# One-hots of the gate spreading shared with GpSimd, key blocks in halves between token groups

## The chip, the cores and the metric

One core of one Trainium2 chip runs the program. The metric is device time in microseconds, the median of several executions. The kernel is written in a low-level language in which each engine has its own instruction stream and waits on semaphores explicitly; nothing reorders what is written. The engines are TensorE (PE), VectorE (DVE), ScalarE (ACT), GpSimd (POOL) and SyncE (SP), which here only issues transfers.

## The reference

It is two sublayers of a decoder for 512 prompt tokens and 32 sample tokens, 544 in all. The first (attention and a state-space mixer) is not touched. The second, PEER, retrieves 16 of 16384 experts for each of 8 heads and token:

```python
def peer_ffn(h, w_q, sub_keys, u_tab, v_tab):
    ...
    s1 = jnp.einsum('nhk,ek->nhe', q[:, :, 0], sk[0])
    s2 = jnp.einsum('nhk,ek->nhe', q[:, :, 1], sk[1])
    v1, i1 = lax.top_k(s1, PEER_TOPK)
    v2, i2 = lax.top_k(s2, PEER_TOPK)
    ...
    expert = jnp.take_along_axis(cidx, top_i, axis=-1)
    gate = jax.nn.softmax(top_s, axis=-1).astype(h.dtype)
    ...
        act = jax.nn.gelu(jnp.einsum('nd,nhkd->nhk', t, u_tab[e]), approximate=False)
        return jnp.einsum('nhk,nhkd->nd', g * act, v_tab[e])
```

An expert's number is 128 a + b, with a the first and b the second key. All is float32.

## The kernel before

384 of the tokens (three tiles of 128) are done densely. For each of the 128 values of a (a "key block") the kernel computes gelu(h U_a) for all 128 experts of the block and all 384 tokens ("up"), writes it to a table `act` in HBM, and later multiplies it with the gates and with V_a ("value"). The other 128 prompt tokens and the 32 sample tokens are done sparsely: their chosen rows of U and V are gathered from HBM (160 gathers of 128 rows of 4 KB for U, 160 for V) and combined on VectorE, a `dot` (L1750) per row of U and a `weighted_row` (L1754) per row of V.

**Up.** A block is 24 matmuls (L188 to L190: high and low halves of both operands, three products, eight chunks). SyncE fetches its 512 KB into `uraw[s]`, one of four slots (`fetch`, L1613); ScalarE casts the high half (`hi_of`, L1390); GpSimd, for the first 83 blocks, or VectorE (L1779) subtracts the low half; TensorE multiplies into bank s; ScalarE applies Gelu (`gelu`, L1662) and SyncE stores the result (`keep`, L1617). 80 blocks run beside the top-k search, and then the slab stage begins.

**Slab stage.** The gates lie as lists (a, b, gate) per token; the value stage wants a dense table gate[b, a, token]. For each token TensorE multiplies two one-hot matrices, `hot_b` (slot against b, times the gate; L1774) by `hot_a` (slot against a; L1773). Four tokens share a bank and form a token group w; there are 96. VectorE makes all one-hots in two buffers (`w % 2`), TensorE writes bank 4 or 5, ScalarE copies the bank into a slab in SBUF (L1695), and when the eight groups of 32 tokens are there SyncE stores the slab, 2 MB, to the table `gate` in HBM (`keep_slab`, L1629). There are 12 slabs. Between the groups TensorE still runs key blocks: four per slab, each followed by two groups (`slab_rows`), 48 in all. VectorE has, per block, two groups of one-hots, the low half of the block three ahead, and one dot (`quarter`). Each engine runs its list in order, so ScalarE's copies stand behind its cast of the block that SyncE fetched after the slab's store.

**Gathers.** GpSimd issues the gathers (L1605) into a ring of eight buffers; each waits until the dot or weighted row of the buffer's last use is done. In the slab stage the ring is filled at once and then four rows per slab are dotted; 16 more follow behind the last slab.

**Value stage.** For each block SyncE loads V_a, and per four blocks the stored activations and gates (`sp_rows`, `sp_gelus`, `sp_gates`). VectorE multiplies activations with gates, splits both operands, and does two sparse rows per block (`pair`); ScalarE casts; TensorE does 18 matmuls of 512 columns. It starts when the last slab is stored and its gates are read back.

The order is written out by hand everywhere; there is no planner. Semaphores count groups: `hot_ready` and `g_done`, `g_kept` tie VectorE, TensorE and ScalarE.

Of the kernel before, what the change touches and what calls it, by code (L numbers as in the profile page):

```python
# [15 lines left out]
P = 128  # L16
# [132 lines left out]
def layer(nc, t):  # L149

    ctx = ExitStack()
    with ctx:
# [1424 lines left out]
        assert EARLY + SLABS * GRP == PK  # L1577
# [8 lines left out]
        hot_ready, g_done, g_kept = (sem(n) for n in ("hot_ready", "g_done", "g_kept"))  # L1586
# [6 lines left out]
        UROWS = SLOTS + SLOTS_S  # L1593

        def pool_gather(pool):
# [4 lines left out]
            for g in range(2 * UROWS):  # L1600
                table, j = tables[g // UROWS], g % UROWS
                at = rows3[:, j:j + 1] if j < SLOTS else rowsS[:, j - SLOTS:j - SLOTS + 1]
                if g >= RING:
                    pool.wait_ge(row_done, g - RING + 1)
                pool.indirect_dma_start(gring[g % RING], None, table, bass.IndirectOffsetOnAxis(ap=at, axis=0)).then_inc(row_in[g % RING], 16)  # L1605

        def sp_up(sp):
# [21 lines left out]
            def keep_slab(n, s):  # L1629
                sp.wait_ge(g_kept, n * GS + (GS + 2))  # L1630
                sp.dma_start(t["gate"][bass.ds(n, 1)].rearrange("s p a n -> p (s a) n"), slab[s]).then_inc(slab_stored[s], 16)

            def last_rows(n, first=False, more=True):
                for s in range(4):
                    if more:
                        a = n * 4 + (EARLY + s + 4)
                        fetch(a, s, (u_lo, QF + EARLY + s + 1) if first and s < LEAD else (u_lo2, n * 4 + (s + 1 - LEAD)))
                    keep(n * 4 + (EARLY + s), s, n + EARLY // 4)

            last_rows(0, True)  # L1640
            with sp.Fori(0, (SLABS - 2) // 2) as x:
                for s in range(2):
                    keep_slab(x * 2 + s, s)
                    last_rows(x * 2 + (s + 1))
            keep_slab(SLABS - 2, 0)
            last_rows(SLABS - 1, more=False)
# [7 lines left out]
            keep_slab(SLABS - 1, 1)  # L1654

        def act_up(act):
# [3 lines left out]
            act.sem_inc(g_kept, 2)  # L1660
# [26 lines left out]
            def last_rows(n, sl, more=True):  # L1687
                for s in range(4):
                    a, q = n * 4 + (EARLY + s), n + EARLY // 4
                    gelu(a, s, q)  # L1690
                    if more:
                        hi_of(act, s, q + (QF // 4 + 1))
                    for par in range(2):
                        act.wait_ge(g_done, n * GS + (2 * s + par + 3))
                        act.copy(slab[sl][:, :, 8 * s + 4 * par:8 * s + 4 * par + 4].rearrange("p a n -> p n a"),  # L1695
                                 bank[:, 4 + par, :].rearrange("p (n a) -> p n a", a=P)).then_inc(g_kept, 1)

            with act.Fori(0, SLABS // 2 - 1) as x:
                for sl in range(2):
                    act.wait_ge(slab_stored[sl], x * 16 + 16)  # L1700
                    last_rows(x * 2 + sl, sl)
            for sl in range(2):
                act.wait_ge(slab_stored[sl], 16 * (SLABS // 2))
                last_rows(SLABS - 2 + sl, sl, sl == 0)


        def pe_up(pe):
# [26 lines left out]
            def slab_rows(n, first=False):  # L1734
                for s in range(4):
                    low = (u_lo, QF + EARLY + s + 1) if first and s < LEAD else (u_lo2, n * 4 + (s + 1 - LEAD))
                    up(n * 4 + (EARLY + s), s, low)
                    for par in range(2):
                        w = n * GS + (2 * s + par)
                        pe.wait_ge(hot_ready, w + 1)  # L1740
                        pe.wait_ge(g_kept, w + 1)
                        for j in range(4):
                            mm = pe.matmul(bank[:, 4 + par, j * P:(j + 1) * P], hot_b[:, par, j], hot_a[:, par, j], start=True, stop=True)  # L1743
                        mm.then_inc(g_done, 1)

            slab_rows(0, True)
            with pe.Fori(1, SLABS) as n:
                slab_rows(n)
# [10 lines left out]
        SLAB_ROWS = SLABS * 4  # L1759

        def dve_onehots(dve):
# [4 lines left out]
            def quarter(x, n2, s, last):  # L1766
                m = x * 8 + (4 * n2 + s)
                for par in range(2):
                    w = x * (2 * GS) + (n2 * GS + 2 * s + par)
                    dve.wait_ge(g_done, w + 1)  # L1770
                    for j in range(4):
                        at = lambda row: slotT[:, row, bass.ds(w * 4 + j, 1)]
                        dve.tensor_scalar(hot_a[:, par, j], const("iota"), at(0), None, ALU.is_equal)  # L1773
                        mm = dve.tensor_scalar(hot_b[:, par, j], const("iota"), at(1), at(2), ALU.is_equal, ALU.mult)  # L1774
                    mm.then_inc(hot_ready, 1)
# [339 lines left out]
```

## Time and profile before

| | |
|---|---|
| median of 3 runs | 2459.61 us (2459.4 to 2464.25) |
| profiled execution | 2450.02 us, span 2448.2 us |
| TensorE matmul busy | 2136.1 us (87%) |
| VectorE busy | 1589.4 us (65%) |
| ScalarE busy | 745.8 us (30%) |
| GpSimd busy | 802.8 us (33%) |
| mean granted TensorE clock | 0.931 |
| moved by DMA | 682.70 MB, mean 279 GB/s |

Shares are of the span of one profiled execution, on the only core. The engines run side by side, so busy times do not add up to the span; where one waits for another is seen in the waits and the timeline of a stretch.

### The profile page before, as it was taken

The page shows a single profiled execution, that of the slowest core. Times are in us where ns is not written, and L with a number is a line of the kernel's source. Part 1 is how long each engine was busy: PE and PEld are TensorE (multiplying, and loading weights), DVE is VectorE, ACT ScalarE, POOL GpSimd, SP SyncE. Part 2 cuts the span into 40 slices and gives each one's busy share as a digit, 9 for nine tenths or more (in the row PEclk, how much of TensorE's full clock was granted, in tenths as well). Part 3 has the DMA queues.
Part 4 walks back from the last instruction along what each step waited for, and adds up shares of the span by engine and source line. Part 5 has one row for each costly group of instructions (what it writes and reads, how often), then busy time and mean ns, then how long its engine had stood idle before and what let it go on. Part 6 is the DMA issues. An engine that isn't in the chain of part 4 may idle for free.

```text
span 2448.2 us, 36552 instructions
## 1 busy us (share of the span) xinstructions
PE 2136.1 (87%) x12253; PEld 1777.8 (73%) x12253; DVE 1589.4 (65%) x3547; ACT 745.8 (30%) x1111; POOL 802.8 (33%) x499
## 2 busy tenths in 40 slices
PE   7978999998769979999999888888399898988984
PEld 7978985554433449999999888888377676776763
DVE  1256125555352331299988677877699898988988
ACT  2123113433330012244344444444132232322231
POOL 2323310001100013366666511111444345665650
PEclk9999998999879989999999998998699899999997
DMA  9999987876995462155555666766899999999992
GB/s 350 352 355 355 356 307 307 325 298 214 325 332 180 165 213 79 43 176 170 173 169 173 218 236 230 251 236 232 322 373 394 391 395 393 395 394 394 395 389 100
DMA packets 200412, 682.70 MB, mean 279 GB/s; under 512 B 18432, under 2 KB 84352, under 8 KB 194304
## 3 DMA queue, kind: packets, MB, share of 16 engines
q1 hardware_dynamic: 151696, 508.36, 58.1%
q0 software_dynamic: 46080, 167.79, 18.1%
q10 hardware_dynamic: 2544, 5.48, 0.6%
q8 instruction: 38, 0.62, 0.1%
q14 instruction: 54, 0.44, 0.1%
HBM read 618.78 MB, written 196.32 MB: 333 GB/s over the span
## 4 chain that ended last, share of the span: by engine, by line
PE 35%; issue 22%; DMA 22%; DVE 12%; ACT 3%; POOL 3%; SPq 1%; DVEq 0%; ACTq 0%; POOLq 0%
DMA overlay<-peer_v 13%; PE bank L188 8%; PE bank L189 8%; PE bank L190 8%; DMA overlay<-peer_u 5%; DVE arena L1757 4%; PE bank L1743 2%; DVE overlay L1912 2%; POOL overlay L341 2%; PE bank L602 2%; POOL overlay L1401 2%; PE bank L586 2%; DVE arena L1752 1%; DMA overlay<-w_in 1%; PE bank L652 1%
## 5 line engine op out<-in xcount | busy, mean ns | idle before, releaser
L188 PE MATMUL bank<-overlay 128*128 128x384 f32 (+4 forms) x2856 | 987.7, 346 | 156.4 <-DVE overlay L1915 109.2
L189 PE MATMUL bank<-overlay 128*128 128x384 f32 (+4 forms) x2856 | 971.5, 340 | 0.0
L190 PE MATMUL bank<-overlay 128*128 128x384 f32 (+4 forms) x2856 | 968.6, 339 | 0.0
L188 PEld LDWEIGHTS bank<-overlay 128*128 128x128 f32 x2856 | 559.2, 196 | 211.7 <-issue 128.4
L190 PEld LDWEIGHTS bank<-overlay 128*128 128x128 f32 x2856 | 557.5, 195 | 33.6
L189 PEld LDWEIGHTS bank<-overlay 128*128 128x128 f32 x2856 | 559.1, 196 | 31.0
L1401 POOL TENSOR_TENSOR overlay<-overlay 128x1024 fp32r<-128x1024 f32 x99 | 268.1, 2711 | 205.7 <-ACT overlay L1393 205.5
L1605 POOL DMA_INDIRECT arena<-peer_rows,arena x160 | 167.3, 1046 | 447.5 <-DVE arena L1752 429.4
L1605 POOL DMA_INDIRECT arena<-peer_v,arena x160 | 236.3, 1477 | 168.8 <-DVE arena L1757 151.5
L1752 DVE SCALAR_TENSOR_TENSOR arena<-arena 128x1024 f32<-128x1024 f32 x160 | 193.9, 1216 | 17.3 <-DMA arena<-peer_rows,arena 17.2
L1757 DVE SCALAR_TENSOR_TENSOR arena<-arena 128x1024 f32<-128x1024 f32 x160 | 204.0, 1275 | 0.0
L1854 ACT CAST overlay<-overlay 128x1024 fp32r<-128x1024 f32 x128 | 134.1, 1048 | 159.3 <-DMA overlay<-peer_v 152.0
L1393 ACT CAST overlay<-overlay 128x1024 fp32r<-128x1024 f32 x144 | 150.6, 1048 | 102.2 <-DMA overlay<-peer_u 99.8
L1912 DVE TENSOR_TENSOR overlay<-overlay 128x1024 fp32r<-128x1024 f32 x128 | 155.6, 1216 | 37.5 <-ACT overlay L1854 37.5
L341 POOL TENSOR_TENSOR overlay<-overlay 128x1024 fp32r<-128x1024 f32 x44 | 104.8, 2393 | 225.8 <-ACT overlay L315 225.8
L1856 ACT CAST overlay<-overlay 128x384 fp32r<-128x384 f32 x128 | 65.7, 513 | 319.3 <-DVE overlay L1908 319.3
L1743 PE MATMUL bank<-arena 128*128 128x128 f32 x768 | 109.9, 304 | 46.7 <-ACT arena L1695 41.9
L1665 ACT ACTIVATE arena<-bank 128x384 f32<-128x384 f32 x128 | 63.5, 496 | 279.7 <-PE bank L190 274.3
L1743 PEld LDWEIGHTS bank<-arena 128*128 128x128 f32 x768 | 106.0, 217 | 50.3 <-issue 44.9
L1773 DVE TENSOR_SCALAR arena<-arena 128x128 f32<-128x128 f32 x384 | 109.0, 284 | 35.1 <-PE bank L1743 24.3
L1774 DVE TENSOR_SCALAR arena<-arena 128x128 f32<-128x128 f32 x384 | 130.6, 340 | 0.0
L1251 PE MATMUL bank<-arena 128*128 128x512 f32 x256 | 116.1, 604 | 0.0
(221 smaller groups left out, 2072.9 us busy)
## 6 DMA issues: line engine op xcount, KB each, us to landing
overlay<-peer_u SPq DMA_DIRECT2D x128, 512.0 KB, 3.6
overlay<-peer_v SPq DMA_DIRECT2D x128, 512.0 KB, 12.8
o_ks<-cache_k SPq DMA_DIRECT2D x16, 4088.0 KB, 26.3
o_vsall<-cache_vall SPq DMA_DIRECT2D x16, 4088.0 KB, 37.9
arena<-cache_kT SPq DMA_DIRECT2D x32, 896.0 KB, 10.9
arena<-cache_v SPq DMA_DIRECT2D x56, 512.0 KB, 6.3
arena<-w_out SPq DMA_DIRECT2D x48, 512.0 KB, 4.7
act<-arena SPq DMA_DIRECT2D x128, 192.0 KB, 1.9
```

The lines of the kernel that those rows point to most:

```text
L188: pe.matmul(out, lhs[0], rhs[0], start=start, stop=False)
L189: pe.matmul(out, lhs[0], rhs[1], start=False, stop=False)
L190: return pe.matmul(out, lhs[1], rhs[0], start=False, stop=stop)
L341: pool.tensor_tensor(ws[1][:, s], wraw[:, s], ws[0][:, s].bitcast(F32), ALU.subtract).then_inc(w_lo, 1)
L1393: act.copy(us[0][:, s], uraw[s]).then_inc(u_hi, 1)
L1401: pool.tensor_tensor(us[1][:, s], uraw[s], us[0][:, s].bitcast(F32), ALU.subtract).then_inc(u_lo, 1)
L1605: pool.indirect_dma_start(gring[g % RING], None, table, bass.IndirectOffsetOnAxis(ap=at, axis=0)).then_inc(row_in[g % RING], 16)
L1743: mm = pe.matmul(bank[:, 4 + par, j * P:(j + 1) * P], hot_b[:, par, j], hot_a[:, par, j], start=True, stop=True)
L1752: dve.scalar_tensor_tensor(gring[r], gring[r], 1.0, h, ALU.mult, ALU.mult, accum_out=w[:, bass.ds(j, 1)]).then_inc(row_done, 1)
L1757: dve.scalar_tensor_tensor(acc, gring[r], w[:, bass.ds(j, 1)], acc, ALU.mult, ALU.add).then_inc(row_done, 1)
L1854: act.copy(vs[0][:, j], vraw[:, k]).then_inc(v_hi, 1)
L1912: dve.tensor_tensor(vs[1][:, j], vraw[:, k], vs[0][:, j].bitcast(F32), ALU.subtract).then_inc(v_lo, 1)
```

## The change

GpSimd makes the `hot_a` one-hots (new semaphore `place_ready`), with the gathers placed between groups; VectorE keeps `hot_b`. Token groups use four banks (4 to 7) instead of two. A slab holds three key blocks instead of four, each in two halves of 12 matmuls, in the order of `ORDER_IN_SLAB`: a tuple ("u", k, half) is half of block k, a number is a token group. The remaining 12 blocks run behind the last slab. VectorE dots five rows per slab and two per block behind, 84 before the value stage instead of 64; the remaining 236 are spread evenly over the 128 blocks of the value stage, whose loop on VectorE is unrolled, as are those of the slab stage on all engines. SyncE loads the first gates (`sp_gates`) during the 12 blocks. The removed lines are those of the kernel above and are mostly cut here.

```diff
@@ -1574,7 +1574,9 @@
 
         AHEAD = 16
         EARLY, SLABS = AHEAD * TILES, DEN // SLAB
-        assert EARLY + SLABS * GRP == PK
+        UPS = 3
+        TAIL = EARLY + SLABS * UPS
+        ORDER_IN_SLAB = (("u", 0, 0), 0, ("u", 0, 1), 1, 2, ("u", 1, 0), 3, ("u", 1, 1), 4, 5, ("u", 2, 0), 6, ("u", 2, 1), 7)
         LEAD = 3
         slab = [cut(10, PK, SLAB), cut(26, PK, SLAB)]
         aring = cut(66, 4, DEN)
...
+        place_ready, hot_ready, g_done, g_kept = (sem(n) for n in ("place_ready", "hot_ready", "g_done", "g_kept"))
...
         GS = SLAB // 4
         GROUPS = PK // GRP
         UROWS = SLOTS + SLOTS_S
+        ROW_TURNS = (1, 2, 4, 5, 7)
+        SLAB_ROWS, TAIL_ROWS = SLABS * len(ROW_TURNS), (PK - TAIL) * 2
 
         def pool_gather(pool):
             pool.wait_ge(topk.sem, after["topk"])
             pool.wait_ge(ch_turned, DT + 1)
             pool.wait_ge(folded, 16 * 2 * FOLD)
             tables = (t["peer_rows"], t["peer_v"].rearrange("a p n -> (a p) n"))
-            for g in range(2 * UROWS):
+
+            def gather(g):
                 table, j = tables[g // UROWS], g % UROWS
                 at = rows3[:, j:j + 1] if j < SLOTS else rowsS[:, j - SLOTS:j - SLOTS + 1]
                 if g >= RING:
                     pool.wait_ge(row_done, g - RING + 1)
                 pool.indirect_dma_start(gring[g % RING], None, table, bass.IndirectOffsetOnAxis(ap=at, axis=0)).then_inc(row_in[g % RING], 16)
+
+            pool.wait_ge(ch_kept, DT + 1)
+            for w in range(SLABS * GS):
+                pool.wait_ge(g_done, w + 1)
+                for j in range(4):
+                    mm = pool.tensor_scalar(hot_a[:, w % 2, j], const("iota"), slotT[:, 0, w * 4 + j:w * 4 + j + 1], None, ALU.is_equal)
+                mm.then_inc(place_ready, 1)
+                if w < RING:
+                    gather(w)
+                elif w % GS in ROW_TURNS:
+                    gather(RING + (w // GS - 1) * len(ROW_TURNS) + ROW_TURNS.index(w % GS))
+            for g in range(RING + (SLABS - 1) * len(ROW_TURNS), 2 * UROWS):
+                gather(g)
...
+            def keep_slab(n):
+                sp.wait_ge(g_kept, n * GS + (GS + 4))
+                sp.dma_start(t["gate"][n], slab[n % 2]).then_inc(slab_stored[n % 2], 16)
+
+            def next_row(a):
+                if a + 4 < PK:
+                    fetch(a + 4, a % 4, (u_lo, QF + a + 1) if a < EARLY + LEAD else (u_lo2, a - (EARLY + LEAD) + 1))
+                keep(a, a % 4, a // 4)
+
+            for n in range(SLABS):
+                if n:
+                    keep_slab(n - 1)
+                for k in range(UPS):
+                    next_row(EARLY + n * UPS + k)
             sp.wait_ge(slab_stored[0], 16 * (1 + SLABS // 2))
             for k in range(GRP):
                 sp_rows(sp, 0, 0, k)
             sp.wait_ge(hot_ready, DEN // 4)
+            sp.wait_ge(place_ready, DEN // 4)
             for s in range(4):
                 sp.wait_ge(a_stored[s], 32)
             sp_gelus(sp, 0, 0)
...
+            keep_slab(SLABS - 1)
+            for a in range(TAIL, PK):
+                next_row(a)
+                if a == TAIL + 3:
+                    sp.wait_ge(slab_stored[1], 16 * (1 + SLABS // 2))
+                    sp_gates(sp, 0, 0)
 
...
+            def next_row(a):
+                gelu(a, a % 4, a // 4)
+                if a + 4 < PK:
+                    hi_of(act, a % 4, (QF + a) // 4 + 1)
+
+            for n in range(SLABS):
+                act.wait_ge(slab_stored[n % 2], 16 * (n // 2 + 1))
+                for what in ORDER_IN_SLAB:
+                    if isinstance(what, tuple):
+                        if what[2] == 1:
+                            next_row(EARLY + n * UPS + what[1])
+                        continue
+                    w = n * GS + what
+                    act.wait_ge(g_done, w + 3)
+                    act.copy(slab[n % 2][:, :, 4 * what:4 * what + 4].rearrange("p a n -> p n a"),
+                             bank[:, 4 + w % 4, :].rearrange("p (n a) -> p n a", a=P)).then_inc(g_kept, 1)
+            for a in range(TAIL, PK):
+                next_row(a)
...
+            def half_up(a, k):
+                s = a % 4
+                if k == 0:
+                    pe.wait_ge(*((u_lo, QF + a + 1) if a < EARLY + LEAD else (u_lo2, a - (EARLY + LEAD) + 1)))
+                    pe.wait_ge(gelu_done, a + 1)
+                for c in range(k * DC // 2, (k + 1) * DC // 2):
+                    mm = product(pe, bank[:, s, 0:DEN], [w[:, s, c] for w in us], [h[:, c, 0:DEN] for h in hh], c == 0, c == DC - 1)
+                if k == 1:
+                    mm.then_inc(u_done, 1)
+
+            for n in range(SLABS):
+                for what in ORDER_IN_SLAB:
+                    if isinstance(what, tuple):
+                        half_up(EARLY + n * UPS + what[1], what[2])
+                        continue
+                    w = n * GS + what
+                    pe.wait_ge(place_ready, w + 1)
+                    pe.wait_ge(hot_ready, w + 1)
+                    pe.wait_ge(g_kept, w + 1)
+                    for j in range(4):
+                        mm = pe.matmul(bank[:, 4 + w % 4, j * P:(j + 1) * P], hot_b[:, w % 2, j], hot_a[:, w % 2, j], start=True, stop=True)
+                    mm.then_inc(g_done, 1)
+            for a in range(TAIL, PK):
+                for k in range(2):
+                    half_up(a, k)
...
+            def low(a):
+                if EARLY + LEAD <= a < PK:
+                    dve.wait_ge(u_hi, QF + a + 1)
+                    dve.tensor_tensor(us[1][:, a % 4], uraw[a % 4], us[0][:, a % 4].bitcast(F32), ALU.subtract).then_inc(u_lo2, 1)
+
+            for n in range(SLABS):
+                for k in range(GS):
+                    w = n * GS + k
                     dve.wait_ge(g_done, w + 1)
                     for j in range(4):
...
+                        at = lambda row: slotT[:, row, w * 4 + j:w * 4 + j + 1]
+                        mm = dve.tensor_scalar(hot_b[:, w % 2, j], const("iota"), at(1), at(2), ALU.is_equal, ALU.mult)
                     mm.then_inc(hot_ready, 1)
...
+                    if k in (0, 3, 6):
+                        low(EARLY + n * UPS + k // 3 + LEAD)
+                    if k in ROW_TURNS:
+                        g = n * len(ROW_TURNS) + ROW_TURNS.index(k)
+                        dot(dve, g % RING, g // RING, h1[:, DT], w3, g)
+            for a in range(TAIL, PK):
+                low(a + LEAD)
+                for k in range(2):
+                    g = SLAB_ROWS + (a - TAIL) * 2 + k
+                    dot(dve, g % RING, g // RING, h1[:, DT], w3, g)
 
 
...
+        DONE = SLAB_ROWS + TAIL_ROWS
+        LATE_ROWS = 2 * UROWS - DONE
...
             for s in range(4):
                 sp.wait_ge(a_stored[s], 16 * (GROUPS + 1))
             sp.wait_ge(u_done, PK)
-            sp_gates(sp, 0, 0)
 
...
+            def late_row(r):
+
+                g = j = DONE + r
+                if j == UROWS:
+                    dve.wait_ge(acc_zeroed, 2)
+                    gate_rows(1, w3, gate3)
+                if j == UROWS + SLOTS:
+                    dve.wait_ge(folded, 16 * 2 * FOLD)
+                    gate_rows(2, wS, gateS)
+                if j < SLOTS:
+                    dot(dve, g % RING, g // RING, h1[:, DT], w3, j)
+                elif j < UROWS:
+                    if j == SLOTS:
+                        dve.wait_ge(h_folded, 16 * (FOLD - 1))
+                    dot(dve, g % RING, g // RING, h1[:, QT], wS, j - SLOTS)
+                elif j < UROWS + SLOTS:
+                    weighted_row(dve, g % RING, g // RING, acc3, w3, j - UROWS, g)
+                else:
+                    weighted_row(dve, g % RING, g // RING, accS, wS, j - UROWS - SLOTS, g)
+
+            for a in range(PK):
+                par, k, j = a // GRP % 2, a % GRP, a % 8
+                rows_here = range(a * LATE_ROWS // PK, (a + 1) * LATE_ROWS // PK)
+                if k == 0:
+                    dve.wait_ge(a_in[par], 16 * (a // 8 + 1))
+                    dve.wait_ge(gate_in[par], 16 * (a // 8 + 1))
+                dve.wait_ge(ga_lo, a + 1)
+                dve.tensor_tensor(prod[j % 2].rearrange("p (s n) -> p s n", n=SLAB),
+                                  agrp[par][:, k].rearrange("p (s n) -> p s n", n=SLAB),
+                                  ggrp[par].rearrange("p (s a n) -> p s a n", a=GRP, n=SLAB)[:, :, k], ALU.mult).then_inc(weighted, 1)
+                dve.wait_ge(v_hi, a + 1)
+                dve.tensor_tensor(vs[1][:, j], vraw[:, k], vs[0][:, j].bitcast(F32), ALU.subtract).then_inc(v_lo, 1)
+                for r in rows_here[0:1]:
+                    late_row(r)
+                dve.wait_ge(ga_hi, a + 1)
+                dve.tensor_tensor(ga[1][:, j], prod[j % 2], ga[0][:, j].bitcast(F32), ALU.subtract).then_inc(ga_lo, 1)
+                for r in rows_here[1:]:
+                    late_row(r)
 
 
```

## Rows read from the trace of the kernel before

**Rows 1.** Windows: the slab stage and the 40 us behind it.
```profile
core 0: us, PE busy (x) PEld busy (x) DVE busy (x) ACT busy (x) POOL busy (x), PEclk, DMA share, GB/s
1374.00:1735.00 361.00, 311.36 (x1920) 307.62 (x1920) 288.79 (x918) 159.79 (x189) 58.77 (x58) 0.92 0.68 236
1735.00:1775.00 40.00, 0.00 (x0) 0.00 (x0) 19.41 (x33) 2.50 (x3) 18.17 (x16) 0.50 1.03 393
```

**Rows 2.** Windows: nine slab periods, and the value stage.
```profile
1418.76:1690.79 272.03, 234.53 (x1440) 231.89 (x1440) 215.95 (x684) 122.13 (x146) 34.13 (x36) 0.91 0.67 234
1775.00:2404.00 629.00, 560.95 (x2278) 446.89 (x2279) 563.61 (x731) 189.28 (x256) 326.70 (x248) 0.94 1.02 385
```

**Rows 3.** Waits, 1374 to 1735 us: total, times, longest.
```profile
ACT overlay L1393 <- DMA overlay<-peer_u: 76.1, 13, 7.9
...
PE bank L1743 <- ACT arena L1695: 41.9, 10, 4.7
```

**Rows 4.** Timeline of one slab: start us, us, engine, line, what, idle before.
```profile
1496.76 0.42 PE L188 MATMUL bank<-overlay 128*128 128x384 f32 x1
...
1498.80 0.33 SPq L1631 DMA_DIRECT2D gate<-arena  x1
1499.42 0.35 SPq L1615 DMA_DIRECT2D overlay<-peer_u  x1
...
1499.77 0.28 DVE L1773 TENSOR_SCALAR arena<-arena 128x128 f32<-128x128 f32 x1
1499.97 0.34 DVE L1774 TENSOR_SCALAR arena<-arena 128x128 f32<-128x128 f32 x1
1500.22 0.28 DVE L1773 TENSOR_SCALAR arena<-arena 128x128 f32<-128x128 f32 x1
...
1501.06 1.95 PE L1743 MATMUL bank<-arena 128*128 128x128 f32 x16
...
1502.76 0.42 PE L188 MATMUL bank<-overlay 128*128 128x384 f32 x1
...
1504.21 1.00 POOL L1605 DMA_INDIRECT arena<-peer_rows,arena  x1 [6.73 <-DVE arena L1752]
...
1506.88 0.34 PE L190 MATMUL bank<-overlay 128*128 128x384 f32 x1
...
1509.77 1.04 ACT L1393 CAST overlay<-overlay 128x1024 fp32r<-128x1024 f32 x1 [7.93 <-DMA overlay<-peer_u]
...
1510.85 1.23 DVE L1779 TENSOR_TENSOR overlay<-overlay 128x1024 fp32r<-128x1024 f32 x1 [3.29 <-ACT overlay L1393]
...
1511.92 3.75 PE L1743 MATMUL bank<-arena 128*128 128x128 f32 x16 [4.70 <-ACT arena L1695]
```

**Rows 5.** Timeline, 1388 to 1394 us: a gather beside VectorE.
```profile
1390.92 3.14 POOL L1605 DMA_INDIRECT arena<-peer_rows,arena  x1 [0.30 <-issue]
1392.04 1.21 DVE L1752 SCALAR_TENSOR_TENSOR arena<-arena 128x1024 f32<-128x1024 f32 x1
```

**Rows 6.** Groups of GpSimd over the span, by form; mean ns after the comma.
```profile
L910 POOL TENSOR_TENSOR arena<-arena 128x256 f32<-128x256 f32 x2 | 1.4, 718 | 0.0
...
L906 POOL TENSOR_TENSOR arena<-arena 32x128 f32<-32x128 f32 x1 | 0.4, 394 | 0.0
...
L332 POOL MEMSET overlay<- 128x96 f32 x1 | 0.2, 178 | 0.4 <-POOLq L2096 0.4
```

**Rows 7.** Timeline, 1350 to 1363 us: VectorE and GpSimd with two inputs each.
```profile
1353.80 4.38 DVE L1542 TENSOR_TENSOR arena<-arena 128x2048 f32<-128x2048 f32 x1
1356.27 4.17 POOL L1401 TENSOR_TENSOR overlay<-overlay 128x1024 fp32r<-128x1024 f32 x1 [0.24 <-ACT overlay L1393]
...
1361.32 2.39 POOL L1401 TENSOR_TENSOR overlay<-overlay 128x1024 fp32r<-128x1024 f32 x1 [0.88 <-ACT overlay L1393]
```

**Rows 8.** DMA issues, 1374 to 1735 us: KB each, median us to landing.
```profile
gate<-arena SPq DMA_DIRECT2D x12, 2048.0 KB, 8.0
overlay<-peer_u SPq DMA_DIRECT2D x43, 512.0 KB, 6.4
act<-arena SPq DMA_DIRECT2D x48, 192.0 KB, 3.9
```

More of the change, by code:

```diff
@@ L1627, in sp_up @@
                     keep(x * 4 + s, s, x)
[L1629 to L1646, printed above, removed]
+            def keep_slab(n):
[10 more added lines that the diff above has]
+                    next_row(EARLY + n * UPS + k)
             sp.wait_ge(slab_stored[0], 16 * (1 + SLABS // 2))
@@ L1659, in act_up @@
             act.sem_inc(gelu_done, 4)
-            act.sem_inc(g_kept, 2)
+            act.sem_inc(g_kept, 4)
             def gelu(a, s, q):
@@ L1732, in pe_up @@
             pe.wait_ge(ch_kept, DT + 1)
[L1734 to L1748, printed above, removed]
+            def half_up(a, k):
[22 more added lines that the diff above has]
+                    half_up(a, k)
         def dot(dve, r, turn, h, w, j):
@@ L1775, in quarter @@
                     mm.then_inc(hot_ready, 1)
-                if not (last and 4 * n2 + s + LEAD >= 8):
-                    u = (s + LEAD) % 4
-                    dve.wait_ge(u_hi, m + (QF + EARLY + LEAD + 1))
-                    dve.tensor_tensor(us[1][:, u], uraw[u], us[0][:, u].bitcast(F32), ALU.subtract).then_inc(u_lo2, 1)
-                dot(dve, 4 * n2 + s, x, h1[:, DT], w3, m)
-            with dve.Fori(0, SLABS // 2 - 1) as x:
-                for n2 in range(2):
-                    for s in range(4):
-                        quarter(x, n2, s, False)
@@ L1786, in dve_onehots @@
-            for n2 in range(2):
-                for s in range(4):
-                    quarter(SLABS // 2 - 1, n2, s, True)
-            for g in range(SLAB_ROWS, SLAB_ROWS + 2 * RING):
-                dot(dve, g % RING, g // RING, h1[:, DT], w3, g)
+                    if k in (0, 3, 6):
[3 more added lines that the diff above has]
+                        dot(dve, g % RING, g // RING, h1[:, DT], w3, g)
@@ L1856, in pair @@
                     act.copy(ga[0][:, j], prod[j % 2]).then_inc(ga_hi, 1)
-            with act.Fori(0, U3_PAIRS + 1) as x:
+            with act.Fori(0, 4) as x:
                 pair(x)
@@ L1861, in act_values @@
             act.activation(w3, w3, ACT.Gelu).then_inc(w_gelu, 1)
-            with act.Fori(U3_PAIRS + 1, US_PAIRS + 1) as x:
+            with act.Fori(4, 6) as x:
                 pair(x)
@@ L1865, in act_values @@
             act.activation(wS, wS, ACT.Gelu).then_inc(w_gelu, 1)
-            with act.Fori(US_PAIRS + 1, PAIRS) as x:
+            with act.Fori(6, PAIRS) as x:
                 pair(x)
```

63 lines of the change are left out of this document (1 added, 62 removed).

## Prediction, made before the changed kernel ran

> **What bounds the kernel now.** I cut the span by stage first, with the view that gives each engine's busy time, the granted clock and the DMA share of a stretch [rows 1, 2]. The change lies in two stages: the slab stage, 1374 to 1735 us (12 slabs, 48 key blocks), and the value stage behind it, which has run from 1775 to 2404 us. In the value stage DMA is the bound: share 1.02 at 385 GB/s in rows 2, and in the 40 us between the two stages, where TensorE does nothing, DMA is full too (1.03, 393 GB/s in rows 1). That gap is therefore not free time: its bytes must be moved anyway. The slab stage is the only one with room: DMA share 0.68 at 236 GB/s, TensorE 311 of 361 us, VectorE 289, clock 0.92 [rows 1].
>
> Nine slabs from 1418.76 to 1690.79 us take 272.03 us [rows 2], 30.2 us each (361 / 12 = 30.1 over all). One slab of the timeline [rows 4] shows what sets them. A block of 24 matmuls runs from 1502.76 to 1506.88, 4.2 us; 16 records of L1743, two token groups, take 1.95 us, so 0.97 a group. Four blocks and eight groups are 16.8 + 7.8 = 24.6 us of TensorE; 5.6 us are lost. SyncE issues the 2 MB store of the previous slab at 1498.80 and the fetch of the next block behind it at 1499.42; ScalarE can cast that block only at 1509.77. ScalarE works in order, so its copies of the group banks wait behind this cast; with two banks TensorE stands until 1511.92 and then does two groups in 3.75 us instead of 1.95, at the lower of its two clocks. The sums over the stage agree: ScalarE waits 76.1 us for peer_u, TensorE 41.9 us for ScalarE's copies [rows 3].
>
> **What the change does to TensorE and VectorE.** TensorE's work moves, none goes: a slab now holds three blocks and eight groups, 12.6 + 7.8 = 20.4 us, and 12 blocks (50 us) run behind the last slab. VectorE loses 32 plain one-hots (L1773) per slab, whose pitch is 0.20 us (1499.77 to 1499.97), and keeps 32 weighted ones at 0.25 us (to 1500.22) [rows 4]. With three lows at 1.2 and five dots at 1.2 [rows 4, 5] (one low fewer, one dot more than before) its slab is 8 + 3.6 + 6 = 17.6 us. That fits beside TensorE's 20.4. Four banks allow TensorE and ScalarE to be four groups apart instead of two.
>
> **What stays: a loop through the store.** The store of slab n-1 waits for ScalarE's last copy; the fetch of the fourth block on is queued behind it; VectorE splits that block behind group 3 and makes group 4's one-hots only after that. Rows 4 price it: store issue to cast 11.0 us, cast 1.0, low 1.3; one-hots of groups 4 to 7 with two dots and one low between them 4.1 + 3.6 = 7.7; group 7, copy and issue 2.4. That is 23.4 us. One gather more falls into the landing, 128 rows of 4 KB or 0.52 MB, 1.3 us at the 393 GB/s of rows 1: 24.7. TensorE meanwhile has four half blocks and four groups, 12.3 us, against the 13 to 16 us until group 4 is ready, so a shorter stall than before stays each slab, with its low clock.
>
> **What GpSimd gets: the unknown price.** It had four gathers of 1.00 us [rows 4] per slab; now five, and 32 tensor_scalars of 128x128, whose price c no row shows. Below stands the memset of 128x96, 0.178 us, which reads nothing; above, the two-input TENSOR_TENSOR of 32x128, 0.394, which has the same 128 columns, and farther off that of 128x256, 0.718 [rows 6]. One input and a per-partition scalar lie under two inputs: I take 0.35, nearest to 0.394. Then GpSimd has 11.2 + 5 x 1.3 (1.0 and the gap of 0.3 of rows 5) = 17.7 us per slab; at 0.178 it is 12.2, at 0.718 29.5.
>
> It does not have them undisturbed. At 1353.80 VectorE starts a two-input op and GpSimd's subtraction of 1356.27 takes 4.17 us instead of 2.39: it ends 2.26 us after VectorE's end at 1358.18 [rows 7]. So one waits for the other wholly. A gather that begins as a low and a dot begin (1390.92) takes 3.14 us instead of 1.00 [rows 4, 5]. Lows and dots are two-input ops, 8 x 1.2 = 9.6 us per slab, so GpSimd's 17.7 (16.2 without the gaps) and VectorE's 9.6 add up: 25.8 to 27.3 us, as long as the loop with its three waits of up to 0.35 for a GpSimd op (25.8). **I take a slab period of 26.5 us**; the bounds on c give 22 (where the loop holds it at 24.7) and 29.5 + 9.6 = 39.
>
> Do the one-hots that VectorE keeps shut GpSimd out too? The gather of 1504.21, in the middle of sixteen one-hots, took 1.00 us [rows 4], so I count nothing; if they did, their 8 us would add to GpSimd's period (rival 2). The Trainium skill speaks for such a lock: "VectorE: DVE Perf Modes" (The perf-mode tier table) lets an fp32 tensor_scalar run at 2x through both ports, and "SBUF — State Buffer" (Who interferes with whom) says that such an op holds the pair shared with GpSimd for the whole instruction. The pitch of 0.20 us in the row is what the cycle table of the former page's errata section gives at 1x (58 + 128 cycles at 0.96 GHz, 0.194 us; 0.127 at 2x), so row and table together speak against 2x here.
>
> **Bytes behind the slabs.** Since DMA bounds all that follows, I count bytes. From 1374 to 2404 us before: 361 us at 236, 40 at 393, 629 at 385 GB/s = 85.2 + 15.7 + 242.2 = 343 MB. After, slabs 0 to 11 carry 36 fetches of 0.52 (18.9), 36 stores of act of 0.2 (7.1), 11 slab stores of 2.1 MB (23.1) and 63 gathers (8 + 11 x 5; 33.0): 82 MB (sizes: [rows 8], with 0.2 MB of act a block). Left for the tail of 12 blocks and the value stage: 261 MB. Before it was 258 MB in 40 + 629 = 669 us, 386 GB/s; at that rate 261 take 676 us. So the tail's 50 us of TensorE work, the 20 rows that are dotted earlier (48 + 16 before, 60 + 24 now) and the closed gap gain nothing by themselves: they only keep TensorE from being late in a stretch that DMA fills. Everything hangs on the slab period.
>
> **Sum.** 12 x 26.5 + 676 = 994 us against 361 + 669 = 1030: 36 us less. The profiled execution took 2450.02 us (span 2448.2), so 2414; the median of the runs is 9.6 us above it, and I carry that over: 2424. Each microsecond of slab period is 12 us; no gain at (1030 - 676) / 12 = 29.5 us. New waits: TensorE's on place_ready before each group, with the half blocks queued behind it, is in the GpSimd figure. The first gathers now go out between one-hots and not at once, but the first dot waits for its landing as before. In the tail the fetch of the ninth block ahead stands behind four peer_v rows, one act group and the last slab store, 5 MB or 13 us, against 17 us of four blocks already fetched: covered, or 2 us. The unrolled loops I cost at nothing; if code were fetched late it would be seen as TensorE's sequencer idle.
>
> **Rivals.**
> 1. *GpSimd becomes the bound.* It needs c above 0.42: 32 x 0.42 + 6.5 + 9.6 = 29.5 us. With c = 0.6 the period is 35.3: 424 + 676 - 1030 = +70 us, 2530; at the far bound, 39, it is +114 us. For it: 0.394 for two inputs is near the threshold, on a quarter of the partitions. Against: one input less. 14%.
> 2. *VectorE's one-hots lock GpSimd out as well*, and it them: 26.5 + 8 = 34.5 us, +60, 2520. Against: the gather of 1504.21; for it: that gather is one op, and 32 per slab are to be placed. 6%. This is what the two pages named above would make of it.
> 3. *The store loop alone decides, the port costs little.* GpSimd's ops slip between VectorE's and the landing stays near 10 us: period 23.5, 282 + 676 = 958, -72 us, 2388. 15%.
> 4. *The change moves the wait only.* More bytes in less time (82 MB in 318 us, 258 GB/s) lengthen the landing by 3 us, and the lower clock stays longer: period 29.5, no gain, 2460. For it: the landing is the largest term of the loop. 7%.
> 5. My forecast, periods 24.5 to 29: 58%, alone 2400 to 2454.
>
> A change within 0.2% (5 us) can't be told from none. Faster by more: 58 + 15, less an edge, 72%; same 7%; slower 21%. The range goes from beyond rival 3 to a period of 31.5 (+24 us), 2372 to 2484; of rivals 1 and 2 most stays outside.
>
> **What would show it.** Slab period: the distance between slab stores (gate<-arena), 26.5 us; above 29.5 I am wrong in sign. GpSimd's one-hots: start-to-start 0.35 us, and lows or dots that last up to 0.35 us more than 1.2. The wait for peer_u at ScalarE should stay, some 3 to 8 us per slab, and TensorE's wait for ScalarE's copies go. If TensorE waits for GpSimd instead, rival 1 holds. From the last slab on DMA should stand at 385 GB/s or more without a gap of TensorE, and last 670 to 682 us; a shorter stretch would prove my count of bytes wrong.

## The result: 2.4% slower, in the slab stage

The changed kernel takes 2519.56 us (median of 4, 2515.02 to 2529.86) against 2461.93 of the kernel before in the same comparison; the ratio is 1.024, with a 95% interval of 1.0205 to 1.0275. The prediction said 2424 us and a range of 2372 to 2484. The time is beside rival 1 (GpSimd as the bound, 2530 us).

The profiled execution (2515.02 us) first as a page: GpSimd's busy time rose from 803 to 1133 us, and on the chain of waits its two lines stand for 14% of the span.

```profile
span 2513.2 us, 34730 instructions
PE 2175.3 (87%) x12253; PEld 1808.0 (72%) x12253; DVE 1545.3 (61%) x3163; ACT 752.9 (30%) x1111; POOL 1132.8 (45%) x883
...
DMA overlay<-peer_v 16%; POOL arena L1616 12%; PE bank L188 6%; PE bank L189 6%; PE bank L190 6%; DVE arena L1787 2%; DVE overlay L1962 2%; POOL arena L1610 2%; POOL overlay L341 2%; PE bank L602 2%; DMA overlay<-peer_u 2%; PE bank L586 2%; POOL overlay L1401 1%; PE bank L652 1%; PE bank L625 1%
```

The same cut by stages as in [rows 1, 2]: slabs, the 12 blocks behind them with the start of the value stage, and the value stage. The columns are those of rows 1.

```profile
1385.00:1783.00 398.00, 298.93 (x1618) 284.00 (x1619) 241.77 (x531) 150.79 (x167) 383.51 (x448) 0.85 0.60 204
1783.00:1857.00 74.00, 53.89 (x293) 52.64 (x291) 39.90 (x59) 16.49 (x24) 38.75 (x28) 0.89 0.96 353
1857.00:2465.00 608.00, 545.27 (x2263) 436.58 (x2264) 540.44 (x692) 189.62 (x256) 312.63 (x230) 0.95 1.03 388
```

In the slab stage GpSimd (the fifth busy figure) is busy 384 of 398 us, VectorE 242, TensorE 299 at a granted clock of 0.85; DMA has fallen from 0.68 to 0.60. Behind it DMA is full, as before. From the first token group to the last it is 1388.9 to 1783.2 us, 394 us (1378.7 to 1732.2, 353.5, before), 41 more; from there to TensorE's last value matmul 692 us (678 before), 14 more. Of the other 10 of the 65 us between the two profiles, 7 lie ahead of all that was changed: the end of the top-k search comes at 1373.6 instead of 1366.6 us, and in the 14 profiles of this study, of kernels that are the same up to there, it lies between 1365.1 and 1378.9. Three lie between it and the first group.

The stores of the slabs, first and eleventh (the first column is the start in us), give the period: (1751.36 - 1423.08) / 10 = 32.8 us, against 30.3 before.

```profile
1423.08 0.34 SPq L1649 DMA_DIRECT2D gate<-arena  x1
...
1751.36 0.33 SPq L1649 DMA_DIRECT2D gate<-arena  x1
```

The waits of the stage (total us, times, longest) show who replaced whom. TensorE's wait for ScalarE's copies, 41.9 us in [rows 3], is gone, and a wait of 100.4 us for GpSimd's one-hots stands in its place. VectorE, the engine that was relieved, waits 88 us for TensorE.

```profile
ACT arena L1721 <- PE bank L1774: 160.7, 53, 9.8
PEld bank L1774 <- POOL arena L1616: 115.5, 56, 5.6
PE bank L1774 <- POOL arena L1616: 100.4, 51, 5.2
DVE arena L1806 <- PE bank L1774: 88.2, 53, 3.2
ACT overlay L1393 <- DMA overlay<-peer_u: 52.4, 11, 5.7
```

What a GpSimd one-hot costs is read from its groups: this is GpSimd's line in the stage (busy, mean ns, idle before) and then its timeline, at the start of the stage and in the middle.

```profile
L1616 POOL TENSOR_SCALAR arena<-arena 128x128 f32<-128x128 f32 x384 | 309.1, 819 | 9.9 <-DMA arena<-arena 7.6
```

```profile
1386.45 2.36 POOL L1616 TENSOR_SCALAR arena<-arena 128x128 f32<-128x128 f32 x4 [7.65 <-DMA arena<-arena]
...
1499.66 6.46 POOL L1616 TENSOR_SCALAR arena<-arena 128x128 f32<-128x128 f32 x8
1506.29 1.97 POOL L1610 DMA_INDIRECT arena<-peer_rows,arena  x1 [0.16 <-issue]
1508.29 3.40 POOL L1616 TENSOR_SCALAR arena<-arena 128x128 f32<-128x128 f32 x4
1511.86 1.03 POOL L1610 DMA_INDIRECT arena<-peer_rows,arena  x1 [0.17 <-issue]
```

Four alone take 2.36 us, 0.59 each; in the mean of the stage an op holds GpSimd for 309.1 / 384 = 0.80 us. VectorE's rows of the same moments show why:

```profile
1499.77 1.35 DVE L1798 TENSOR_TENSOR overlay<-overlay 128x1024 fp32r<-128x1024 f32 x1 [2.08 <-ACT overlay L1393]
1501.05 1.23 DVE L1806 TENSOR_SCALAR arena<-arena 128x128 f32<-128x128 f32 x4
1502.20 1.21 DVE L1782 SCALAR_TENSOR_TENSOR arena<-arena 128x1024 f32<-128x1024 f32 x1
...
1508.05 2.06 DVE L1806 TENSOR_SCALAR arena<-arena 128x128 f32<-128x128 f32 x4 [0.68 <-PE bank L1774]
1510.02 1.21 DVE L1798 TENSOR_TENSOR overlay<-overlay 128x1024 fp32r<-128x1024 f32 x1
```

Eight GpSimd ops from 1499.66 took 6.46 us instead of 4.7, with a low and a dot beside them; four from 1508.29 took 3.40 instead of 2.36, with one low. That is 0.9 to 1.0 us for each two-input op of 1.2 us. The whole stage says the same, read instruction by instruction from the trace: 257 of the 384 ops have no low and no dot beside them and take 0.59 to 0.71 us each, one-hots of VectorE beside them or not; 82 take over 1.2 us, and every one of these has a low or a dot beside it. This is the lock of [rows 7]. Gathers feel it only at times: that of 1506.29, with a dot beside it, took 1.97 us instead of 1.03, but of the 14 gathers of the stage that have a low or a dot beside them for over 0.3 us, five took under 1.15. The parts add up to the period: 32 x 0.80 + 5 x 1.34 (a gather's mean 1.17 and the gap of 0.17 before it) = 32.5 of the 32.8 us.

### The profile page after: what moved, and what is told of

It is laid out like the page before. It is cut to its first block, busy times and chain, and to the rows that moved or that the text cites. A ratio compares the mean times of both kernels' runs of the same rounds, so it can differ in the third digit from the quotient of the medians.

```text
span 2513.2 us, 34730 instructions
## 1 busy us (share of the span) xinstructions
PE 2175.3 (87%) x12253; PEld 1808.0 (72%) x12253; DVE 1545.3 (61%) x3163; ACT 752.9 (30%) x1111; POOL 1132.8 (45%) x883
## 4 chain that ended last, share of the span: by engine, by line
PE 29%; issue 20%; DMA 20%; POOL 17%; DVE 10%; ACT 2%; SPq 0%; ACTq 0%; POOLq 0%; DVEq 0%
DMA overlay<-peer_v 16%; POOL arena L1616 12%; PE bank L188 6%; PE bank L189 6%; PE bank L190 6%; DVE arena L1787 2%; DVE overlay L1962 2%; POOL arena L1610 2%; POOL overlay L341 2%; PE bank L602 2%; DMA overlay<-peer_u 2%; PE bank L586 2%; POOL overlay L1401 1%; PE bank L652 1%; PE bank L625 1%
## 5 line engine op out<-in xcount | busy, mean ns | idle before, releaser
L188 PE MATMUL bank<-overlay 128*128 128x384 f32 (+4 forms) x2856 | 1000.2, 350 | 130.0 <-DVE overlay L1966 69.5
L189 PE MATMUL bank<-overlay 128*128 128x384 f32 (+4 forms) x2856 | 982.3, 344 | 0.0
L190 PE MATMUL bank<-overlay 128*128 128x384 f32 (+4 forms) x2856 | 980.0, 343 | 0.0
L188 PEld LDWEIGHTS bank<-overlay 128*128 128x128 f32 x2856 | 568.5, 199 | 183.4 <-issue 84.9
L190 PEld LDWEIGHTS bank<-overlay 128*128 128x128 f32 x2856 | 566.9, 199 | 32.7
L189 PEld LDWEIGHTS bank<-overlay 128*128 128x128 f32 x2856 | 568.1, 199 | 30.3
L1616 POOL TENSOR_SCALAR arena<-arena 128x128 f32<-128x128 f32 x384 | 309.1, 819 | 9.9 <-DMA arena<-arena 7.6
L1610 POOL DMA_INDIRECT arena<-peer_rows,arena x160 | 186.2, 1164 | 153.0 <-DVE arena L1782 132.8
L1774 PE MATMUL bank<-arena 128*128 128x128 f32 x768 | 122.7, 309 | 100.5 <-POOL arena L1616 100.4
L1806 DVE TENSOR_SCALAR arena<-arena 128x128 f32<-128x128 f32 x384 | 133.8, 438 | 95.0 <-PE bank L1774 88.2
L1721 ACT COPY arena<-bank 128x512 f32<-128x512 f32 x96 | 103.6, 1101 | 160.7 <-PE bank L1774 160.7
```

Of the source, the lines that this page charges most:

```text
L188: pe.matmul(out, lhs[0], rhs[0], start=start, stop=False)
L189: pe.matmul(out, lhs[0], rhs[1], start=False, stop=False)
L190: return pe.matmul(out, lhs[1], rhs[0], start=False, stop=stop)
L1616: mm = pool.tensor_scalar(hot_a[:, w % 2, j], const("iota"), slotT[:, 0, w * 4 + j:w * 4 + j + 1], None, ALU.is_equal)
L1774: mm = pe.matmul(bank[:, 4 + w % 4, j * P:(j + 1) * P], hot_b[:, w % 2, j], hot_a[:, w % 2, j], start=True, stop=True)
```

## Experiments

Theory A: GpSimd's work per slab, 32 ops and five gathers, sets the period. Theory B: the new order (three blocks in halves, four banks, 12 blocks behind) costs the time. Periods are from the first to the eleventh slab store; ratios are to the kernel before, run beside, with 95% intervals.

**All one-hots back on VectorE.** GpSimd's loop over the groups goes, with `place_ready`; it only issues gathers.

```diff
-            for w in range(SLABS * GS):
-            ...
-            for g in range(RING + (SLABS - 1) * len(ROW_TURNS), 2 * UROWS):
+            for g in range(2 * UROWS):
                 gather(g)
...
+                        dve.tensor_scalar(hot_a[:, w % 2, j], const("iota"), at(0), None, ALU.is_equal)
                         mm = dve.tensor_scalar(hot_b[:, w % 2, j], const("iota"), at(1), at(2), ALU.is_equal, ALU.mult)
```

> The changed kernel with all one-hots on VectorE again; everything else of the change stays (three blocks per slab in halves, four banks, 12 blocks behind). Theory A (the one-hots on GpSimd set the slab period, 33.1 us): the period falls to what VectorE and the loop through the store allow, 25 to 28 us, and the 5 us in which the first group waited for GpSimd go: 2520 - 12 x 6.6 - 5 = 2436 us, 2420 to 2455, faster than the kernel before (2462). Theory B (the new order of blocks, banks and stores costs the time, GpSimd's waits only show it): 2505 to 2530.

Measured 2439.8 us, ratio 0.9924 (0.9895 to 0.9954), period 27.7 us. A holds, B falls: the rest of the change is a gain of 0.8%, and the part on GpSimd turns it into a loss.

**The GpSimd part alone, in the kernel before.**

```diff
+            for w in range(SLABS * GS):
+                pool.wait_ge(g_done, w + 1)
+                for j in range(4):
+                    mm = pool.tensor_scalar(hot_a[:, w % 2, j], const("iota"), slotT[:, 0, w * 4 + j:w * 4 + j + 1], None, ALU.is_equal)
+                mm.then_inc(place_ready, 1)
+                if w < RING: gather(w)
+                elif w % 2 == 1: gather(RING + (w - 9) // 2)
...
-                        dve.tensor_scalar(hot_a[:, par, j], const("iota"), at(0), None, ALU.is_equal)
```

> The kernel before with one part of the change: GpSimd makes the plain one-hots, four gathers per slab between the groups. Theory A: GpSimd has 32 x 0.8 + 4 x 1.35 = 31 us per slab against the 29.9 of before, and the first group waits 5 us more: 2462 + 19 = 2481 us, 2470 to 2495. Theory B: VectorE is relieved of 6.4 us per slab, so 2440 to 2462.

Measured 2471.06 us, 1.0052 (1.0034 to 1.007), period 30.4 us, GpSimd's mean op 0.78 us. As A said, and a little less: with four gathers and dots instead of five GpSimd needs just what the slab took before.

**One op more per group.**

```diff
+                    if j == 2:
+                        pool.tensor_scalar(spare[:, w % 6], const("iota"), slotT[:, 0, w * 4 + j:w * 4 + j + 1], None, ALU.is_equal)
```

> The changed kernel with a fifth one-hot per group on GpSimd, written to a spare tile that nobody reads. Theory A: 96 ops lie on the path: 96 x 0.6 to 0.9 = 58 to 86 us more, 2578 to 2606. Theory B or any other bound: GpSimd has slack, under 10 us more, below 2530.

Measured 2565.24 us, 1.0436 (1.0396 to 1.0476); the period grew from 32.8 to 37.55 us, 4.7 for eight ops: 0.59 us each. All 96 lie on the path, at the price of an op alone, since the number of two-input ops that hold GpSimd up stayed the same. The total grew by 46 us, 11 less than 12 x 4.7 and under what A expected (2578 to 2606). From the first to the last token group it is 449.0 us, 54.7 more, nearly the whole 12 x 4.7; the rest of the 11 us lies outside the stage and is not explained.

**No dots in the slab stage.**

```diff
-        ROW_TURNS = (1, 2, 4, 5, 7)
+        ROW_TURNS = ()
```

(ScalarE's two Gelus of the dots move two pairs back, since the dots come later.)

> The changed kernel without dots (and without all but the first eight gathers) in the slab stage; they follow in the value stage, which has 296 rows instead of 236. Theory A1 (GpSimd's op takes 0.6 us alone and 0.8 in the mean because VectorE's two-input ops shut it out): with five of eight such ops gone the mean start-to-start falls to 0.65 to 0.70 us, the slab period to 22 to 24 us. Theory A2 (0.8 us whatever VectorE does with two inputs): 0.8 us and 26 us or more. The time: slabs carry 29 MB less, which DMA has to move behind them at 386 GB/s, 75 us, so 2520 - 12 x 10 + 75 = 2475 by A1 and 2510 by A2.

Measured 2485.5 us, 1.0112 (1.007 to 1.0153), period 23.3 us. GpSimd's line, 1400 to 1700 us:

```profile
L1616 POOL TENSOR_SCALAR arena<-arena 128x128 f32<-128x128 f32 x375 | 249.7, 683 | 21.0 <-PE bank L1774 20.7
```

The mean op fell from 819 to 683 ns, 32 x 0.136 = 4.4 us per slab for five dots fewer; five gathers of 1.2 gone too make it 10.4 against the 9.5 us that the period fell by. The lock (A1) is shown: the run took dots and gathers away together, but of its 384 ops 34 took over 1.2 us, about as many as there are lows, and all of them have a low or a dot beside them. A2's 0.8 us whatever VectorE does is out. The slabs gave 12 x 9.5 = 114 us, but from the last group to the last value matmul it is 767 us instead of 692: the 75 us for 29 MB came back as counted, since DMA bounds what follows.

**Half the columns.** The other 64 columns stay zero (one memset ahead), so this kernel leaves out half of the gates.

```diff
-                    mm = pool.tensor_scalar(hot_a[:, w % 2, j], const("iota"), slotT...
+                    mm = pool.tensor_scalar(hot_a[:, w % 2, j, 0:64], const("iota")[:, 0:64], slotT...
```

> The changed kernel with GpSimd's one-hots 64 columns wide instead of 128 (the other columns stay zero, so half of the gates are left out; one memset ahead). If the 0.58 us of an op alone is mostly a fixed cost, it falls to 0.50 to 0.55 and the period to 31: 2490 to 2510. If it goes with the columns, it falls to 0.30 and the period to that of all one-hots on VectorE or below, 25 to 27 us: 2430 to 2450.

Measured 2446.96 us, 0.9969 (0.9946 to 0.9992), period 27.8 us. A group alone:

```profile
1384.94 1.70 POOL L1619 TENSOR_SCALAR arena<-arena 128x64 f32<-128x64 f32 x4
```

0.42 us an op instead of 0.59: the price of neither case, though the time lies in the range of the second. A line through the two widths, an estimate, gives 0.25 us fixed and 2.7 ns a column. What ends the period at 27.8 is not settled. The loop through the store gives 27.7 with all one-hots on VectorE, and ScalarE's wait for peer_u is nearly the same here (53.5 us from 1400 to 1700, against 57.3). But GpSimd is still busy 286 of these 300 us, since its mean op holds it for 0.62 us beside the lows and dots, and TensorE waits 54.3 us for it. The two bounds lie too close together for this run to part them.

**Two of four on GpSimd.**

```diff
-                for j in range(4):
+                for j in range(2):
...
+                        if j >= 2:
+                            dve.tensor_scalar(hot_a[:, w % 2, j], const("iota"), at(0), None, ALU.is_equal)
```

> The changed kernel with GpSimd making two of the four plain one-hots of each group and VectorE the other two. If GpSimd's price is 0.8 us an op and otherwise harmless, it has 16 x 0.8 + 5 x 1.4 = 19.8 us per slab and VectorE 20.8: period 26 to 27 us (27.7 with all on VectorE, 32.8 with all on GpSimd), a few us under the time with all on VectorE: 2430 to 2440. If the two engines' ops hold each other up, and not GpSimd's sum of work alone, the period stays at 27.7 or above: 2445 or more.

Measured 2440.53 us, 0.9939 (0.9914 to 0.9963), period 27.4: the same as with all on VectorE, and between the two cases (26 to 27, or 27.7 and above). What VectorE was spared it spent waiting: from 1400 to 1700 us it waits 57.8 us for ScalarE's casts ahead of its lows, against 38.2 with all one-hots. So VectorE's work did not bound that kernel. What does, the next run asks.

**The fetch ahead of the store**, with all one-hots on VectorE:

```diff
-                if n:
-                    keep_slab(n - 1)
                 for k in range(UPS):
-                    next_row(EARLY + n * UPS + k)
+                    a = EARLY + n * UPS + k
+                    if k == 0 and n:
+                        fetch(a + 4, ...)
+                        keep_slab(n - 1)
+                        keep(a, a % 4, a // 4)
+                    else:
+                        next_row(a)
```

> All one-hots on VectorE, and SyncE issues the first fetch of each slab ahead of the 2 MB store of the slab before, not behind it. Theory L (the loop store, fetch, cast, low, one-hots sets the 27.7 us): the period falls to VectorE's 24 to 25 us and ScalarE's wait for peer_u nearly goes: 12 x 3 = 36 us less than 2440, 2395 to 2412. Theory V (VectorE in turn with TensorE sets 27.7 us already): less than 8 us, 2432 to 2445.

Measured 2398.23 us, 0.9767 (0.9715 to 0.9818), period 23.6 us; theory L. The window over ten periods has VectorE busy all the time:

```profile
1408.00:1651.00 243.00, 208.54 (x1398) 204.31 (x1397) 243.00 (x792) 132.44 (x145) 138.68 (x51) 1.00 0.82 292
```

**Both.**

> Two of four plain one-hots on GpSimd and the fetch ahead of the store. Under theory L with work shared: 22 to 23.5 us a slab (TensorE has 20.4), 2375 to 2400. If GpSimd and VectorE hold each other up: 25 us or more, no better than the fetch ahead of the store with all one-hots on VectorE.

Measured 2400.14 us, 0.9777 (0.9746 to 0.9808), period 23.65: not better, although VectorE was the bound and lost half of its plain one-hots; the period of neither case. VectorE is again busy without a break (236 of 236 us from 1404 to 1640, GpSimd 226), and the line of its weighted one-hots (here and in the run before, 1400 to 1640 us) shows where the relief went:

```profile
L1799 DVE TENSOR_SCALAR arena<-arena 128x128 f32<-128x128 f32 x325 | 107.1, 329 | 0.0
...
L1812 DVE TENSOR_SCALAR arena<-arena 128x128 f32<-128x128 f32 x326 | 147.4, 475 | 0.0
```

The mean op grew from 329 to 475 ns. By its prices VectorE has 32 x 0.25 + 16 x 0.20 + 8 x 1.2 = 20.8 us per slab; it took 23.65. The 2.8 us more, nearly all of the 3.2 that VectorE was relieved of, come from GpSimd's ops beside it, the only thing that the edit added. TensorE meanwhile waited 30 us of 240 for GpSimd: the two full engines hold each other up.

**The changed kernel with the fetch ahead of the store** (the same edit).

> The changed kernel, all plain one-hots on GpSimd, with the first fetch of each slab ahead of the store. Theory A (GpSimd's 32 ops and 5 gathers set the 32.8 us): the change that took 4.1 us a slab off the kernel with all one-hots on VectorE takes under 1 here, 2508 to 2525. If the loop through the store has part in the 32.8 us, it falls by 2 to 4 us a slab: 2470 to 2495.

Measured 2512.49 us, 1.0216 (1.0192 to 1.024), period 32.79 against 32.83. The edit that took 4.1 us a slab off the kernel with VectorE's one-hots does nothing here, although ScalarE's wait for peer_u fell from 43.2 to 0.2 us (1400 to 1700 us): the loop had no part in the 32.8 us.

**The kernel before with the fetch ahead of the store.**

```diff
-            def last_rows(n, first=False, more=True):
+            def last_rows(n, first=False, more=True, store=None):
                 for s in range(4):
                     if more: fetch(...)
+                    if s == 0 and store:
+                        keep_slab(*store)
                     keep(...)
...
-                    keep_slab(x * 2 + s, s)
-                    last_rows(x * 2 + (s + 1))
+                    last_rows(x * 2 + (s + 1), store=(x * 2 + s, s))
```

> The kernel before with the fetch ahead of the store alone. If the loop through the store set its 30.3 us, the period falls to TensorE's 24.6 us and some waits, 25.5 to 27: with the bytes behind the slabs unchanged, 12 x 4 = 40 to 55 us less, 2402 to 2417, about the time that the changed order with all one-hots on VectorE and this fetch has (2398). If two banks or the whole blocks had part in it: 28 us or more, 2430 or more.

Measured 2392.56 us, 0.9735 (0.9706 to 0.9765), period 24.3 us: below what was expected (25.5 to 27, 2402 to 2417) and the lowest median of all, 4.9% under the changed kernel (0.9735 / 1.024), from one pair of transfers in the other order. Its interval overlaps with that of the changed order with all one-hots on VectorE and the same fetch (0.9767), so once the fetch goes first, nothing is left of the 0.8% of the first experiment. Window and waits:

```profile
1408.00:1651.00 243.00, 241.56 (x1603) 240.50 (x1602) 236.41 (x761) 136.69 (x160) 40.02 (x40) 1.00 0.82 291
```

```profile
ACT overlay L1393 <- DMA overlay<-peer_u: 24.0, 10, 4.3
```

TensorE is busy 241.6 of 243 us at the full clock (0.91 in [rows 2]) and waits for nobody's copies; the 24.6 us of TensorE's work that the prediction counted for such a slab is its period.

**Two banks**, and **whole blocks**, both with all one-hots on VectorE:

```diff
-                        mm = pe.matmul(bank[:, 4 + w % 4, ...
+                        mm = pe.matmul(bank[:, 4 + w % 2, ...
```

(ScalarE's copy and the counts of `g_kept` go with it.)

> All one-hots on VectorE, order of the changed kernel, two banks instead of four. In the kernel before TensorE waited 42 us for ScalarE's copies; if four banks removed that, it comes back in part: period 28.5 to 30, 2448 to 2465. If the one-hots, which VectorE holds back behind the same block, end the wait anyway: within 5 us of 2440.

Measured 2439.33 us, 0.9926 (0.9902 to 0.995), period 27.0. Four banks are worth nothing in this kernel.

```diff
-        ORDER_IN_SLAB = (("u", 0, 0), 0, ("u", 0, 1), 1, 2, ("u", 1, 0), 3, ("u", 1, 1), 4, 5, ("u", 2, 0), 6, ("u", 2, 1), 7)
+        ORDER_IN_SLAB = (("u", 0, 0), ("u", 0, 1), 0, 1, 2, ("u", 1, 0), ("u", 1, 1), 3, 4, 5, ("u", 2, 0), ("u", 2, 1), 6, 7)
```

> All one-hots on VectorE, four banks, but each block's two halves together (u0, 0, 1, 2, u1, 3, 4, 5, u2, 6, 7). TensorE then has the two blocks and four groups ahead of group 4 as before, so the loop through the store is unchanged: within 8 us of 2440. If the halves were what gained over the kernel before: 2450 or more.

Measured 2429.48 us, 0.9893 (0.9864 to 0.9922), period 26.55: just outside the 8 us, on the fast side, so halves gain nothing either. Its interval touches that of the halves. So the 0.8% of the first experiment comes from neither banks nor halves. Three blocks instead of four per slab are left, with the dots and the first gates that moved with them; no run changed one of these alone, and it stays open.

## Why the prediction was wrong

The step that failed is one term: the price c of a GpSimd one-hot, "I take 0.35, nearest to 0.394". It is 0.59 us alone. The bound from the two-input op of 32x128 was no bound: another operation on a quarter of the partitions says nothing of this one, and the far end, 0.718 for 256 columns, was the side to lean to. With 0.59 in its own formula the prediction has 32 x 0.59 + 6.5 + 9.6 = 35 us per slab; measured were 32.8, against the 26.5 forecast. The rest, point by point:

- *Lock between two-input ops and GpSimd*: right in kind (the 82 long ops, and the run without dots), too large in sum. Eight two-input ops were counted at 9.6 us per slab; the mean op is 0.80 - 0.59 = 0.21 us longer, 32 x 0.21 = 6.7, and the mean gather 0.14 longer, 0.7 for five.
- *VectorE's kept one-hots and GpSimd do not disturb each other*: right for GpSimd, whose ops beside them took at most 0.71 us (rival 2 did not come), wrong for VectorE. A group of four took 1.23 us at 1501.05, where 4 x 0.25 was counted; that of 1508.05, which began under a gather, took 2.06, its first three ops 0.6 us apart, GpSimd's own pitch. In the changed kernel VectorE also waits 88 us for TensorE, and no run separates how much of this lies on the path there; with the fetch ahead and VectorE as the bound it was 2.8 us per slab. By the Trainium skill ("SBUF — State Buffer", Who interferes with whom) a VectorE op in a two-port mode and a GpSimd op shut each other out for the whole instruction, and a VectorE op with two inputs in SBUF contends with a GpSimd op that reads SBUF. The dots and lows, which have two inputs, behave like the latter, at 0.9 to 1.0 us for 1.2; the one-hots at 1501.05 do not behave like the former, since they ran beside GpSimd ops of 0.59 us and lost 0.2.
- *The loop through the store, 24.7 us plus what VectorE adds*: right, and the best part. With all one-hots on VectorE (3.2 us more behind the wait) it gives 27.9; measured 27.7. The fetch ahead of the store confirms it in two kernels. It did not decide the changed kernel, because GpSimd was longer.
- *TensorE's waits for copies go*: right (41.9 us in [rows 3], not among the waits after), as one bound gave way to a longer one.
- *The bytes behind the slabs*: right that DMA bounds them and that little is gained or lost, but short. From the last group to the last value matmul it is 678 us before, 692 after, 691 with VectorE's one-hots and 677 in the kernel with 48 blocks in the slabs and the fetch ahead; the forecast was 676 against 669. The stretch was to last 670 to 682 us; the kernels of the changed order with dots in the slabs have 686 to 702. The 12 blocks behind, the earlier rows and the closed gap gain nothing, as said; they lose some 7 us more than counted. TensorE waits 12 us behind the last slab for a block fetched after the store (22 us from its fetch at 1787.36 to its cast at 1809.79, where the sum had 13 and called it covered); that this wait is the loss is likely and not shown.
- *Each microsecond of slab period is 12 us*: right. The 65 us between the profiles are 41 in the slabs (25 in the ten periods, 6 in the first slab, 10 in the last), 14 behind them, 7 ahead of all changes and 3 before the first group: its one-hots now wait for the folded lists, which GpSimd's gathers need, and VectorE's did not wait for them (from the end of the search to the first group it is 9.6 to 12.1 us in the profiles with all one-hots on VectorE, 14.1 to 15.7 in those in which GpSimd makes some). These 3 us were missed.

The chances were wrong in the same place: 14% for rival 1 leaned on c, whose bounds straddled the threshold of 0.42. A term with ends of 0.18 and 0.72 and a threshold in their midst should have had nearly even odds.

## What to carry to other kernels

When work moves to an engine for which no row has that operation, set the bounds against the threshold at which the sign turns (here 0.42 us between 0.18 and 0.72, a coin toss) and measure one such op alone before the move. A busy engine is not the bound while a loop of waits ends last: follow it once round (here store, fetch, cast, split, one-hots, copy, store) and try to break it before work is moved. The order of two transfers in one queue, the urgent one first, gave 2.7%, where the redistribution without its GpSimd part gave 0.8% and the GpSimd part lost 3.2%. The next bound may stand close behind the one that is eased: with half-width one-hots GpSimd and the loop through the store lie so near each other, at 27.7 to 27.8 us, that one run can't part them.

## What the hardware showed that I had not expected

A GpSimd tensor_scalar of 128x128 with a scalar per partition takes 0.59 us alone, 2.4 times the 0.25 of VectorE's op with one step more, and 0.42 at 64 columns. One-hots of the two engines slow each other unevenly: VectorE's weighted ones went from 329 to 475 ns in the mean when GpSimd made half of the plain ones (both with the fetch ahead), while GpSimd's, 0.59 us at the least, took at most 0.71 in the changed kernel where no low or dot ran beside them. TensorE's granted clock did not simply follow its idle time. It was 0.85 in the stage in which TensorE waited for GpSimd in group after group (up to 5.2 us at a time) and 0.91 with one stall per slab (up to 4.7 us). It was 1.00 both in the kernel before with the fetch ahead, which has next to no waits, and in the changed order with all one-hots on VectorE and the fetch ahead, where TensorE waited 33 us of 240, but at most 1.7 us at a time.
